# Moving the gating and normalisation of the DeltaNet heads from GpSimd to VectorE

## The chip, the cores and the metric

One core of a Trainium2 chip runs the whole program. The time is the device time of one execution in microseconds; the kernel before takes 1177.71 us, the median of three runs (1175.47 to 1178.70). The engines are TensorE (PE), VectorE (DVE), ScalarE (ACT), GpSimd (POOL) and the DMA queue of SyncE (SP). Each runs its own list of instructions in order and waits for others on semaphores.

## The reference, cut to what matters

Two mixer blocks follow each other. The change lies in the second, a gated DeltaNet over 512 tokens with 16 value heads of width 128. For each head it computes, token by token,

```python
o = ...                                       # chunked delta rule, (tokens, heads, 128)
o = rms_norm_2(o, norm_w) * jax.nn.silu(z)    # per token and head: o * rsqrt(mean(o*o) + 1e-6) * norm_w * silu(z)
y = o.reshape(bsz, t, nh * dh) @ w_out        # (512, 2048) @ (2048, 1024)
x = x + gate * y                              # gate: one row of 1024, from the condition
out = rms_norm_2(x, final_g)
```

All is float32. A float32 product on TensorE is made of three products of rounded high and low parts (`hi` and `lo`); so every weight block is rounded by ScalarE (`hi`) and the rest is subtracted by VectorE or GpSimd (`lo`) before use.

## The kernel before, in words

The second mixer works on two groups (`i` = 0, 1) of four head pairs (`j` = 0 to 3). A pair is walked in four chunks of 128 tokens (`c` = 0 to 3). The order is written out by hand for each engine; nothing plans it.

**A chunk.** PE multiplies with the running state `S`; DVE makes `R` from that (L2597), PE makes `w` (L1904), DVE scales it into `we` and `w_sb` (L2605, L2609), PE makes the state update (L1909) and the output (L1918), and DVE writes the chunk's output into `O[j % 2]` (L2632 or L2634, semaphore `o_ok`). `O` lies in the tile `es`. ACT takes the sum of squares of each output chunk (L2182, `osq_ok`).

**Fills.** Between these steps PE, ACT and DVE do the triangular inverse of the next pair (`doubled` on DVE, L2584 and L2589). The last pair of a group has no next one: there `fill` turns the finished heads, makes their `hi` and `lo` parts (`high`, `low`), and in group 1 begins the output product.

**A finished pair.** GpSimd gates it (`gate_heads`, L2366: z = z * O, 128x1024), makes the factor `rs` from the sums of squares (`norm_factor`, L2351 and L2354), and multiplies (`finish`, L2372: z = z * rs, 128x1024, `z_ok` + 8). `z` lies in the tile `tok`. PE turns heads e = 2j, 2j + 1 only when `z_ok` has their 8 (`turn_m`, L1925).

**GpSimd's other work.** It spreads the inverse's factors (`expand`, L1609), makes the decay steps (L2340, into `es`) and the masked products (L2407), and subtracts weight rests (`out_rest`, L1587, 128x2048).

**The end.** `partial` holds the output product of group 0's heads. GpSimd adds it, times the gate row, to the residual: `add_partial(t)`, two 128x1024 operations for each of four token blocks (L2379, L2381), three of them ahead of the last pair's gating. PE turns e = 14, 15, then needs weight rest 6 (`wo_lo[0]` = 4) for the second half of the output columns and rest 7 (`wo_lo[2]`) for its last quarter. DVE makes rest 6, GpSimd rest 7. DVE adds each finished output block (L2705, L2707).

Of the kernel before, what the change touches and what calls it, by code (L numbers as in the profile page):

```python
# [9 lines left out]
ALU = mybir.AluOpType  # L10
ACT = mybir.ActivationFunctionType

P = 128
# [62 lines left out]
class Phase(ExitStack):  # L76
# [14 lines left out]
    def sem(self, name):  # L91
        s = self.enter_context(self.nc.semaphore(f"{self.name}_{name}"))
        Phase.used.append(s.num)
        return s
# [1299 lines left out]
def second_mixer(nc, a, ahead, wba, wba_in, split, raw, masks, resid, row_f, modc, gain, small, z):  # L1394
# [7 lines left out]
    with ctx:  # L1402
# [150 lines left out]
        osq_ok = sem("osq_ok")  # L1553
        rs_ok = sem("rs_ok")
        heads_out = sem("heads_out")
        z_gated, z_ok = sem("z_gated"), sem("z_ok")
        m_g_in, row_g_in, x_in = sem("m_g_in"), sem("row_g_in"), sem("x_in")
        m_turned, m_hi_ok, m_lo_ok = sem("m_turned"), sem("m_hi_ok"), sem("m_lo_ok")
        wo_in = [sem(f"wo_in{r}") for r in range(2)]
# [522 lines left out]
        def _(act):  # L2082
# [231 lines left out]
            for e in (12, 13):  # L2314
                high(e, 13 - e)
            round_out(6, b_used, 1)
            round_out(7, o_made, NB * HB * TT)
            for e in (14, 15):
                high(e, 15 - e)
            for half_n in range(2):  # L2320
                cols = slice(half_n * COLS, (half_n + 1) * COLS)
                for t in range(TT):
                    n = TT * half_n + t
                    act.wait_ge(added, n + 1)
                    if n:
                        act.wait_ge(sum_ok, n)
                    nc.scalar.activation(scratch[0][:, cols], resid[:, t, cols], ACT.Square, scale=D_MODEL ** -0.5,  # L2327
                                         accum_out=halves[:, half_n, t:t + 1]).then_inc(sum_ok, 1)

        @block.gpsimd  # L2330
        def _(pool):
# [17 lines left out]
            def norm_factor(i, j):  # L2349
# [3 lines left out]
                pool.wait_ge(pool_s, at(i, 1, j, 3))  # L2353
                nc.gpsimd.tensor_tensor(rs[:, j % 2], ms[:],  # L2354
                                        half[:, 1, 0:2 * TT].rearrange("p (h c) -> p h c", c=TT), ALU.pow).then_inc(rs_ok, 1)

            def heads_z(i, j):

                return z[:, :, (i * HB + j) * 2 * P:(i * HB + j + 1) * 2 * P].rearrange("p c (h e) -> p h c e", h=2)

            def gate_heads(i, j):

                pool.wait_ge(o_ok, at(i, 4, j, 4))
                if i == 0 and j == 0:
                    pool.wait_ge(zp_out, TT * B_Z)
                nc.gpsimd.tensor_tensor(heads_z(i, j), heads_z(i, j), O[j % 2], ALU.mult).then_inc(z_gated, 1)  # L2366

            def finish(i, j):

                pool.wait_ge(rs_ok, at(i, 1, j, 1))  # L2370
                pool.wait_ge(z_gated, at(i, 1, j, 1))
                nc.gpsimd.tensor_tensor(heads_z(i, j), heads_z(i, j),  # L2372
                                        rs[:, j % 2].unsqueeze(3).broadcast_to([P, 2, TT, P]), ALU.mult).then_inc(z_ok, 8)

            def add_partial(t):

                if t:
                    pool.wait_ge(part_ok, 2 * t)
                nc.gpsimd.tensor_tensor(gated, partial[:, t, :], row_b, ALU.mult).then_inc(part_ok, 1)  # L2379
                pool.wait_ge(part_ok, 2 * t + 1)  # L2380
                nc.gpsimd.tensor_tensor(resid[:, t, :], resid[:, t, :], gated, ALU.add).then_inc(part_ok, 1)  # L2381

            def begin(i):
                if i:
# [10 lines left out]
            for i in range(NB):  # L2395
                for j in range(HB):
                    if j + 1 < HB:
                        log_decay_steps(i, j + 1)
                    if i and j == HB - 1:
                        out_rest(nc.gpsimd, pool, 3)  # L2400
                    pool.wait_ge(e_ok, at(i, 1, j, 1))
                    pool.wait_ge(kk_out, at(i, 2, j, 2))
                    if i == 0 and j == 0:

                        for b in range(2):
                            pool.wait_ge(spilled[b], 16 * (B_CONV // 2))
                    nc.gpsimd.tensor_tensor(PT[:, 8 * j:8 * j + 8, :].rearrange("p (h c) e -> p h c e", h=2),  # L2407
                                            E.rearrange("p (h c) e -> p h c e", h=2),
                                            KQm.unsqueeze(1).broadcast_to([P, 2, TT, P]), ALU.mult).then_inc(pt_ok, 1)
                pool.wait_ge(kss_ok, at(i, 1, HB - 1, 1))  # L2410
                nc.gpsimd.tensor_tensor(flat(rinv[:]), flat(kss[:]), half[:, 0, :], ALU.pow).then_inc(rinv_ok, 1)
                if i == 0:
                    for s in range(2):
                        w.rest(nc.gpsimd, pool, s, B_CONV + 3)
                pool.wait_ge(uc_ok, i * 2 + 1)
                pool.wait_ge(pt_ok, at(i, 1, HB - 1, 1))
                expand(i, 0, Uc, U[0], ux_ok)
                pool.wait_ge(uc_ok, i * 2 + 2)
                expand(i, 1, Tc, T, tx_ok)
                expand(i, 1, Uc, U[1], ux_ok)  # L2420
                out_rest(nc.gpsimd, pool, 4 * i)
                for j in range(HB):
                    if j:
                        gate_heads(i, j - 1)
                        norm_factor(i, j - 1)
                        finish(i, j - 1)
                    if j + 2 < HB:
                        expand(i, j + 2, Tc, T, tx_ok)
                        pool.wait_ge(w_made, at(i, 4, j, 4))
                        expand(i, j + 2, Uc, U[j % 2], ux_ok)  # L2430
                    if j == 1:
                        out_rest(nc.gpsimd, pool, 4 * i + 1)
                if i == 0:
                    begin(1)
                else:
                    pool.wait_ge(gate_out, 2)
                    pool.wait_ge(x_in, 16)
                    pool.wait_ge(yp_out, 2 * TT)
                    pool.wait_ge(z_ok, 8 * (NB * HB - 1))
                    for t in range(3):  # L2440
                        add_partial(t)
                gate_heads(i, HB - 1)
                norm_factor(i, HB - 1)
                finish(i, HB - 1)

            add_partial(3)
            out_rest(nc.gpsimd, pool, 7)
            for t in range(TT):
                pool.wait_ge(sum_ok, t + 1)
                nc.gpsimd.tensor_scalar(halves[:, 0, t:t + 1], halves[:, 0, t:t + 1], 1.0, EPS2, ALU.mult, ALU.add)\  # L2450
# [10 lines left out]
        def _(dve):  # L2461
# [130 lines left out]
            def chunk_part(i, j, c, fill):  # L2592
# [31 lines left out]
                fill(4 * c + 2)  # L2624
                dve.wait_ge(o_made, at(i, 4, j, c + 1))
                out = O[slot][:, :, c, :]
                if c == 0 and j >= 2:

                    dve.wait_ge(z_gated, at(i, 1, j - 2, 1))
                if c:  # L2630
                    dve.wait_ge(qt_ok, at(i, 6, j, 2 * c))
                    nc.vector.tensor_tensor(out, psO[:, 2:4, :], qt[:], ALU.add).then_inc(o_ok, 1)  # L2632
                else:
                    nc.vector.tensor_copy(out, psO[:, 2:4, :]).then_inc(o_ok, 1)  # L2634
                fill(4 * c + 3)

            def low(e, bank):
                dve.wait_ge(m_hi_ok, e + 1)
# [3 lines left out]
            def heads_of(i):  # L2642
# [21 lines left out]
                for j in range(HB):  # L2664
                    parts = doubling_parts(j + 1) if j + 1 < HB else None

                    def fill(n):
                        if parts:
                            if n < len(parts):
                                doubled(i, j + 1, *parts[n])  # L2670
                        elif n == 2:
                            for e in range(8 * i, 8 * i + 4):
                                low(e, 2 + e % 8)
                        elif i == 0 and n == 5:
                            select(1)
                        elif i and n == 0:
                            nc.vector.tensor_tensor(diag.rearrange("p (k c) -> p k c", c=P),
                                                    ident.unsqueeze(1).broadcast_to([P, KT, P]),
                                                    modc[:, 2 * KT:].unsqueeze(2).broadcast_to([P, KT, P]), ALU.mult)\
                                .then_inc(gate_in, 1)  # L2680

                    for c in range(TT):
                        chunk_part(i, j, c, fill)
                dve.wait_ge(o_ok, at(i, 4, HB - 1, 4))
                dve.sem_inc(heads_out, 1)
                for e in (12, 13) if i else (4, 5):
                    low(e, 13 - e if i else e - 2)

            for i in range(NB):
                heads_of(i)  # L2690
            out_rest(nc.vector, dve, 6)
            for e in (14, 15):
                low(e, 15 - e)

            def finish_row(t, halves=1):
                if t == 0:
# [7 lines left out]
            def add_gated(x, y, gate, n):  # L2704
                own.did(nc.vector.tensor_tensor(scratch[1][:, 0:n], y, gate, ALU.mult))  # L2705
                own.wait()
                return nc.vector.tensor_tensor(x, x, scratch[1][:, 0:n], ALU.add)  # L2707

            for half_n in range(2):
                cols = slice(half_n * COLS, (half_n + 1) * COLS)  # L2710
                for t in range(TT):
                    dve.wait_ge(acc_made, TT * half_n + t + 1)
                    if half_n or t:
                        dve.wait_ge(added, TT * half_n + t)
                    if half_n == 0:
                        dve.wait_ge(part_ok, 2 * (t + 1))
                    add_gated(resid[:, t, cols], ps[:, (2, 3, 4, 5, 6, 7, 0, 1)[TT * half_n + t], :], row_b[:, cols], COLS)\
                        .then_inc(added, 1)
                    if half_n and t in (1, 2):
# [54 lines left out]
```

## Time and profile before

| | |
|---|---|
| median of three runs | 1177.71 us (1175.47 to 1178.70) |
| the profiled execution | 1178.70 us, its span 1176.9 us |
| PE busy | 1117.6 us, 95% |
| DVE busy | 670.5 us, 57% |
| ACT busy | 465.5 us, 40% |
| POOL busy | 244.3 us, 21% |
| TensorE clock granted, mean | 0.982 |

The second mixer's head loops run from about 868 us to 956 us (group 0) and from about 1040 us to 1130 us (group 1); the end follows. A row of the timeline gives start, duration, engine, line, operation, output and inputs, and in brackets how long the engine sat idle before it and what released it. The `x2` or `x8` at a row's end are equal instructions merged into one row, from the first's start to the last's end.

### The profile page before, as it was taken

To read this page: it belongs to the slowest core of one execution; us is meant where nothing else is said; L and a number is where in the kernel's file an instruction comes from. 1 tells how busy PE (TensorE), PEld (TensorE's weight loads), DVE (VectorE), ACT (ScalarE), POOL (GpSimd) and SP (SyncE) were. 2 spreads that over 40 slices of the span, in tenths; PEclk is the share of its full clock that TensorE was granted. 3 is DMA by queue.
4 is the path that set the end of the run, shared out by engine and by line. 5 is a ranking of instruction groups with operands and counts; after the bars stand their busy time and mean duration, and the time that the engine had idled before them with its cause. 6 is when DMAs were issued, how large, how long until landed. Compare 5 with 4: busy or idle time off the path is not lost. (4 is left out here: it accounts for less than half of the span.)

```text
span 1176.9 us, 15099 instructions
## 1 busy us (share of the span) xinstructions
PE 1117.6 (95%) x5878; PEld 926.3 (79%) x5878; DVE 670.5 (57%) x1081; ACT 465.5 (40%) x853; POOL 244.3 (21%) x170
## 2 busy tenths in 40 slices
PE   6999999999899899897999999999999889999897
PEld 4888888888689777786787888777799877788785
DVE  3245437621366877458377576576635667845635
ACT  3222233331466532224233333476245446244531
POOL 0001000000000422012000000133434553436592
PEclk9999999999999899899999999999999989999999
DMA  8276524231310502233243453432211212111401
GB/s 281 74 266 240 172 89 161 72 107 53 126 55 19 184 1 72 91 106 109 84 143 115 165 186 108 142 126 90 72 55 55 90 37 90 36 57 53 161 2 71
DMA packets 58308, 124.06 MB, mean 105 GB/s; under 512 B 5760, under 2 KB 5888, under 8 KB 58112
## 3 DMA queue, kind: packets, MB, share of 16 engines
q1 hardware_dynamic: 55792, 110.22, 27.7%
q0 software_dynamic: 2304, 12.58, 2.9%
q8 instruction: 45, 0.74, 0.3%
q10 hardware_dynamic: 144, 0.33, 0.1%
q14 instruction: 23, 0.19, 0.1%
HBM read 108.96 MB, written 14.16 MB: 105 GB/s over the span
## 5 line engine op out<-in xcount | busy, mean ns | idle before, releaser
L285 DVE TENSOR_TENSOR w_lo<-raw,w_hi 128x2048 fp32r<-128x2048 f32 x56 | 130.3, 2328 | 222.3 <-ACT w_hi L281 211.2
L281 ACT ACTIVATE w_hi<-raw 128x2048 fp32r<-128x2048 f32 x51 | 97.6, 1913 | 228.4 <-PE projections_ps L131 148.3
L129 PE MATMUL projections_ps<-projections_x_hi,w_hi 128*128 128x512 f32 x224 | 88.1, 393 | 3.0 <-DVE w_lo L285 2.6
L131 PE MATMUL projections_ps<-projections_x_hi,w_lo 128*128 128x512 f32 x224 | 87.6, 391 | 0.0
L130 PE MATMUL projections_ps<-projections_x_lo,w_hi 128*128 128x512 f32 x224 | 87.6, 391 | 0.0
L129 PE MATMUL projections_ps<-w_hi,projections_x_hi 128*128 128x512 f32 x192 | 74.7, 389 | 0.0
L130 PE MATMUL projections_ps<-w_lo,projections_x_hi 128*128 128x512 f32 x192 | 74.7, 389 | 0.0
L131 PE MATMUL projections_ps<-w_hi,projections_x_lo 128*128 128x512 f32 x192 | 74.7, 389 | 0.0
L242 DVE SCALAR_TENSOR_TENSOR resid<-resid,mixer_cw 128x512 f32<-128x512 f32 x96 | 65.0, 745 | 0.0
L2340 POOL TENSOR_TENSOR mixer_es<-masks,mixer_gsel 128x1024 f32<-128x1024 f32 x8 | 15.4, 1927 | 235.4 <-DVE mixer_bsel L2511 210.7
L2589 DVE COPY_PREDICATED mixer_space<-mixer_masks,mixer_ps 128x512 f32<-128x512 int32 x48 | 35.6, 742 | 45.7 <-PE mixer_ps L1878 45.7
L129 PE MATMUL mixer_ps<-w_hi,mixer_ha_hi 128*128 128x512 f32 x128 | 55.7, 435 | 5.3 <-ACT tok L2112 2.3
L129 PE MATMUL output_ps<-w_hi,output_m_hi 128*128 128x512 f32 x128 | 54.1, 423 | 0.7 <-DVE output_m_lo L1233 0.6
L1171 POOL MEMSET output_half_neg<- 128x4 f32 x1 | 0.1, 101 | 260.1 <-POOLq L649 260.1
L129 PEld LDWEIGHTS projections_ps<-projections_x_hi,w_hi 128*128 128x128 f32 x224 | 42.4, 189 | 12.5 <-issue 3.1
L129 PE MATMUL mixer_ps<-mixer_ha_hi,w_hi 128*128 128x512 f32 x128 | 50.6, 395 | 0.9 <-DVE w_lo L285 0.5
L131 PE MATMUL mixer_ps<-w_hi,mixer_ha_lo 128*128 128x512 f32 x128 | 51.2, 400 | 0.0
L130 PE MATMUL mixer_ps<-w_lo,mixer_ha_hi 128*128 128x512 f32 x128 | 51.1, 399 | 0.0
L130 PE MATMUL output_ps<-w_lo,output_m_hi 128*128 128x512 f32 x128 | 50.9, 398 | 0.0
L131 PE MATMUL output_ps<-w_hi,output_m_lo 128*128 128x512 f32 x128 | 50.7, 396 | 0.0
L129 PE MATMUL mixer_ps<-mixer_hb_hi,w_hi 128*128 128x512 f32 x128 | 50.4, 394 | 0.0
L1878 PE MATMUL mixer_ps<-mixer_space 128*128 128x128 f32 x384 | 50.4, 275 | 0.0
(314 smaller groups left out, 2765.8 us busy)
## 6 DMA issues: line engine op xcount, KB each, us to landing
raw<-in_w_in SPq DMA_DIRECT2D x26, 1024.0 KB, 5.0
raw<-in_gdn_w_in SPq DMA_DIRECT2D x24, 1024.0 KB, 5.0
tok<-in_ada_w POOLq DMA_DIRECT2D x16, 768.0 KB, 6.3
raw<-in_w_out SPq DMA_DIRECT2D x8, 1024.0 KB, 5.0
qkv_kept<-mixer_ring SPq DMA_DIRECT2D x8, 1024.0 KB, 4.2
mixer_st<-qkv_kept SPq DMA_DIRECT2D x32, 256.0 KB, 3.0
raw<-in_gdn_w_out SPq DMA_DIRECT2D x8, 1024.0 KB, 5.2
resid<-in_att_bias SPq DMA_DIRECT2D x16, 256.0 KB, 2.7
```

The lines of the kernel that those rows point to most:

```text
L129: nc.tensor.matmul(out, w_hi, x_hi, start=first, stop=False, skip_group_check=True)
L130: nc.tensor.matmul(out, w_hi, x_lo, start=False, stop=False, skip_group_check=True)
L131: return nc.tensor.matmul(out, w_lo, x_hi, start=False, stop=last, skip_group_check=True)
L242: ins = nc.vector.scalar_tensor_tensor(out=acc, in0=src, scalar=tap, in1=acc, op0=ALU.mult, op1=ALU.add)
L281: self.nc.scalar.activation(self.hi[s][:], self.raw[s][:], ACT.Copy).then_inc(self.hi_ready, 1)
L285: engine.tensor_tensor(self.lo[s][:], self.raw[s][:], self.hi[s][:], ALU.subtract)\
L1171: nc.gpsimd.memset(half_neg[:], -0.5).then_inc(pool_step, 1)
L1878: mm = nc.tensor.matmul(out, V[:, m, :], U[j % 2][:, m, :], start=True, stop=True)
L2340: nc.gpsimd.tensor_tensor(steps, upper.unsqueeze(1).broadcast_to([P, 8, P]), gs.unsqueeze(2).broadcast_to([P, 8, P]), ALU.mult).then_inc(s ...
L2589: nc.vector.copy_predicated(U[j % 2][:, 4 * grp:4 * grp + 4, :], level.unsqueeze(1).broadcast_to([P, 4, P]), psZ[:, grp, :].rearrange("p ( ...
```

## The change

The two GpSimd passes over z are gone. In their place DVE does eight SCALAR_TENSOR_TENSOR operations of 128x128 for each pair, z = (O * rs) * z, one for each head and chunk; each adds 1 to `z_ok`. DVE does them for pair j - 1 after chunk 1 of pair j (j = 1 to 3), and for the last pair of a group after the two `low` that follow it. GpSimd keeps `norm_factor`. The semaphore `z_gated` goes, and DVE no longer waits for it before it reuses `O`. At the end GpSimd adds `partial` for t = 2 and 3 only, t = 2 after the last pair's `norm_factor`; DVE adds t = 0 and 1 after its last two `low`. Rest 6 goes from DVE to GpSimd, and ACT rounds unit 7 after `high` of 14 and 15.

```diff
@@ ACT, the end
             round_out(6, b_used, 1)
-            round_out(7, o_made, NB * HB * TT)
             for e in (14, 15):
                 high(e, 15 - e)
+            round_out(7, o_made, NB * HB * TT)
@@ GpSimd
                     if j:
-                        gate_heads(i, j - 1)
                         norm_factor(i, j - 1)
-                        finish(i, j - 1)
...
-                    for t in range(3):
-                        add_partial(t)
-                gate_heads(i, HB - 1)
                 norm_factor(i, HB - 1)
-                finish(i, HB - 1)
...
+            pool.wait_ge(z_ok, 8 * (NB * HB - 1))
+            add_partial(2)
+            for v in (6, 7):
+                out_rest(nc.gpsimd, pool, v)
+            pool.wait_ge(part_ok, 2)
             add_partial(3)
-            out_rest(nc.gpsimd, pool, 7)
@@ DVE
-                    dve.wait_ge(z_gated, at(i, 1, j - 2, 1))
...
+            def finish(i, j):
+
+                dve.wait_ge(rs_ok, at(i, 1, j, 1))
+                if i == 0 and j == 0:
+                    dve.wait_ge(zp_out, TT * B_Z)
+                for h in range(2):
+                    for c in range(TT):
+                        at_z = i * (2 * HB * P) + (2 * j + h) * P
+                        zz = z[:, c, at_z:at_z + P]
+                        nc.vector.scalar_tensor_tensor(out=zz, in0=O[j % 2][:, h, c, :], scalar=rs[:, j % 2, h, c:c + 1],
+                                                       in1=zz, op0=ALU.mult, op1=ALU.mult).then_inc(z_ok, 1)
...
                         chunk_part(i, j, c, fill)
+                        if c == 1 and j:
+                            finish(i, j - 1)
...
                     low(e, 13 - e if i else e - 2)
+                finish(i, HB - 1)
...
-            out_rest(nc.vector, dve, 6)
             for e in (14, 15):
                 low(e, 15 - e)
...
+            for t in range(2):
+                own.wait()
+                own.did(add_gated(resid[:, t, :], partial[:, t, :], row_b, D_MODEL))
```

DVE before, around the end of chunk 1 of a pair with j = 1 to 3 (L2619 is the state, L2632 the output of the chunk into `es`, L2597 is `R` of the next chunk):

```order
L2619 SCALAR_TENSOR_TENSOR mixer_S<-mixer_S,mixer_dsel,mixer_ps 128x128 x2
L2632 TENSOR_TENSOR mixer_es<-mixer_ps,mixer_qt 128x2x128
L2597 SCALAR_TENSOR_TENSOR mixer_R<-mixer_ps,mixer_dsel,mixer_vr 128x128 x2
```

The same place after; the lines are numbered anew, L2595, L2605 and L2573 are the three from above:

```order
L2595 SCALAR_TENSOR_TENSOR mixer_S<-mixer_S,mixer_dsel,mixer_ps 128x128 x2
L2605 TENSOR_TENSOR mixer_es<-mixer_ps,mixer_qt 128x2x128
L2619 SCALAR_TENSOR_TENSOR tok<-mixer_es,mixer_rs,tok 128x128 x8
L2573 SCALAR_TENSOR_TENSOR mixer_R<-mixer_ps,mixer_dsel,mixer_vr 128x128 x2
```

The eight new operations stand between a chunk's output and the next chunk's `R`.

GpSimd before, from the gating of pair 2 of group 1 to the last weight rest:

```order
L2366 TENSOR_TENSOR tok<-tok,mixer_es 128x2x4x128
L2351 TENSOR_TENSOR mixer_ms<-mixer_sums,mixer_qe 128x8
L2354 TENSOR_TENSOR mixer_rs<-mixer_ms,mixer_half 128x8
L2372 TENSOR_TENSOR tok<-tok,mixer_rs 128x2x4x128
L2379 TENSOR_TENSOR mixer_es<-tok,mixer_Tc 128x1024
L2381 TENSOR_TENSOR resid<-resid,mixer_es 128x1024
```

(twice more L2379 and L2381, then L2366, L2351, L2354, L2372, L2379, L2381 and rest 7.) After, from the factor of the last pair on:

```order
L2351 TENSOR_TENSOR mixer_ms<-mixer_sums,mixer_qe 128x8
L2354 TENSOR_TENSOR mixer_rs<-mixer_ms,mixer_half 128x8
L2411 TENSOR_TENSOR mixer_es<-tok,mixer_Tc 128x1024
L2413 TENSOR_TENSOR resid<-resid,mixer_es 128x1024
L1587 TENSOR_TENSOR w_lo<-raw,w_hi 128x2048
L1587 TENSOR_TENSOR mixer_w_lo<-raw,mixer_w_hi 128x2048
L2411 TENSOR_TENSOR mixer_es<-tok,mixer_Tc 128x1024
L2413 TENSOR_TENSOR resid<-resid,mixer_es 128x1024
```

The first addition of `partial` now follows the last pair's factor, and rest 6 follows that.

DVE after, from the `low` of 12 and 13 to the first output block; the kernel before has rest 6 where L2619 stands, and neither of the four 128x1024 rows:

```order
L2624 SCALAR_TENSOR_TENSOR mixer_hb_lo<-mixer_ps,mixer_m_g,mixer_hb_hi 128x512 x2
L2619 SCALAR_TENSOR_TENSOR tok<-mixer_es,mixer_rs,tok 128x128 x8
L2624 SCALAR_TENSOR_TENSOR mixer_hb_lo<-mixer_ps,mixer_m_g,mixer_hb_hi 128x512 x2
L2695 TENSOR_TENSOR mixer_ktok<-tok,mixer_Tc 128x1024
L2697 TENSOR_TENSOR resid<-resid,mixer_ktok 128x1024
L2695 TENSOR_TENSOR mixer_ktok<-tok,mixer_Tc 128x1024
L2697 TENSOR_TENSOR resid<-resid,mixer_ktok 128x1024
L2695 TENSOR_TENSOR mixer_ktok<-mixer_ps,mixer_Tc 128x512
```

## Rows read from the trace of the kernel before

**Rows 1.** The page, busy time of the engines.
```profile
PE 1117.6 (95%) x5878; PEld 926.3 (79%) x5878; DVE 670.5 (57%) x1081; ACT 465.5 (40%) x853; POOL 244.3 (21%) x170
```

**Rows 2.** The waits of PE, 860 to 1177 us: total, times, longest.
```profile
PE mixer_ps L1850 <- DVE mixer_space L2589: 4.8, 6, 0.9
```

**Rows 3.** Timeline of DVE, group 0, pair 2, chunks 1 and 2.
```profile
923.61 0.42 DVE L2632 TENSOR_TENSOR mixer_es<-mixer_ps,mixer_qt 128x256 f32<-128x256 f32 x1 [0.73 <-PE mixer_ps L1918]
924.94 0.61 DVE L2597 SCALAR_TENSOR_TENSOR mixer_R<-mixer_ps,mixer_dsel,mixer_vr 128x128 f32<-128x128 f32 x2 [0.90 <-PE mixer_ps L1887]
...
926.89 0.41 DVE L2605 TENSOR_TENSOR mixer_we<-mixer_ps,mixer_wsce 128x256 f32<-128x256 f32 x1
927.22 0.42 DVE L2609 TENSOR_TENSOR mixer_w_sb<-mixer_ps,mixer_wsc 128x256 f32<-128x256 f32 x1
```

**Rows 4.** Timeline of PE, the same chunk.
```profile
926.06 0.61 PE L1904 MATMUL mixer_ps<-mixer_R,mixer_space 128*128 128x128 f32 x4
```

**Rows 5.** Timeline of DVE, two operations with both inputs in SBUF.
```profile
1172.99 1.42 DVE L2701 SCALAR_TENSOR_TENSOR resid<-resid,row_f,mixer_Uc 128x512 f32<-128x512 f32 x2 [0.71 <-POOL row_f L2458]
```

**Rows 6.** Timeline of DVE, group 0, pair 3, chunks 1 and 2.
```profile
944.93 0.42 DVE L2632 TENSOR_TENSOR mixer_es<-mixer_ps,mixer_qt 128x256 f32<-128x256 f32 x1 [0.25 <-PE mixer_ps L1918]
946.00 0.61 DVE L2597 SCALAR_TENSOR_TENSOR mixer_R<-mixer_ps,mixer_dsel,mixer_vr 128x128 f32<-128x128 f32 x2 [0.64 <-PE mixer_ps L1887]
```

**Rows 7.** Timelines of DVE and PE, group 1, pair 3, chunks 1 and 2.
```profile
1119.74 0.42 DVE L2632 TENSOR_TENSOR mixer_es<-mixer_ps,mixer_qt 128x256 f32<-128x256 f32 x1 [0.53 <-PE mixer_ps L1918]
1120.87 0.61 DVE L2597 SCALAR_TENSOR_TENSOR mixer_R<-mixer_ps,mixer_dsel,mixer_vr 128x128 f32<-128x128 f32 x2 [0.70 <-PE mixer_ps L1887]
...
1121.80 0.61 PE L1904 MATMUL mixer_ps<-mixer_R,mixer_space 128*128 128x128 f32 x4
```

**Rows 8.** Timelines of POOL, DVE and PE: group 1, pair 3, start; last, an undisturbed DVE row.
```profile
1107.33 2.37 POOL L2366 TENSOR_TENSOR tok<-tok,mixer_es 128x1024 f32<-128x1024 f32 x1 [10.15 <-DVE mixer_es L2632]
...
1108.19 2.58 DVE L2677 TENSOR_TENSOR mixer_space<-masks,modc 128x1024 f32<-128x1024 f32 x1
...
1111.17 0.70 PE L1909 MATMUL mixer_ps<-mixer_we,mixer_ktok 128*128 128x256 f32 x2 [1.21 <-DVE mixer_we L2605]
...
995.68 1.22 DVE L2540 TENSOR_TENSOR resid<-mixer_space,mixer_nbp 128x1024 f32<-128x1024 f32 x1
```

**Rows 9.** Timelines of POOL, DVE and PE between the two groups.
```profile
960.42 1.90 POOL L2372 TENSOR_TENSOR tok<-tok,mixer_rs 128x1024 f32<-128x1024 f32 x1
...
962.59 1.60 DVE L2526 SCALAR_TENSOR_TENSOR mixer_nbp<-mixer_bsel,mixer_r 128x8 f32<-128x8 f32 x1
...
971.43 1.96 PE L1839 MATMUL mixer_ps<-mixer_es,masks 128*128 128x512 f32 x4 [0.94 <-DVE mixer_hb_lo L2639]
```

**Rows 10.** Timelines of ACT, POOL, DVE and PE at the end.
```profile
1130.31 0.19 ACT L2182 ACTIVATION_READ_ACCUMULATOR mixer_junk<-mixer_es 128x1 f32 x1
...
1134.47 1.92 ACT L2194 ACTIVATE w_hi<-raw 128x2048 fp32r<-128x2048 f32 x1 [2.66 <-PE mixer_ps L131]
...
1134.87 1.64 POOL L2354 TENSOR_TENSOR mixer_rs<-mixer_ms,mixer_half 128x8 f32<-128x8 f32 x1
1136.65 3.82 POOL L2372 TENSOR_TENSOR tok<-tok,mixer_rs 128x1024 f32<-128x1024 f32 x1
...
1136.42 2.29 DVE L1587 TENSOR_TENSOR w_lo<-raw,w_hi 128x2048 fp32r<-128x2048 f32 x1 [3.75 <-ACT w_hi L2194]
...
1140.53 1.09 PE L1925 MATMUL mixer_ps<-masks,tok 128*128 128x128 f32 x8 [0.55 <-POOL tok L2372]
1141.38 0.48 PE L129 MATMUL mixer_ps<-w_hi,mixer_ha_hi 128*128 128x512 f32 x1
```

**Rows 11.** Line L1587 on POOL: duration ns min/median/max, first and last start.
```profile
L1587 POOL TENSOR_TENSOR w_lo<-raw,w_hi x5: 4527/4534/4566, 870.1 to 1086.4; 128x2048 fp32r<-128x2048 f32 x5
```

**Rows 12.** Timeline of PE at its earlier wait for ACT.
```profile
757.52 0.50 PE L129 MATMUL mixer_ps<-w_hi,mixer_ha_hi 128*128 128x512 f32 x1 [2.27 <-ACT tok L2112]
```

**Rows 13.** Windows of PE: stretch, length, busy (count), PEclk, DMA share, GB/s.
```profile
757.00:767.00 10.00, 9.48 (x43) 0.83 0.37 135
```

More of the change, by code:

```diff
@@ L1555, in second_mixer @@
         heads_out = sem("heads_out")
-        z_gated, z_ok = sem("z_gated"), sem("z_ok")
+        z_ok = sem("z_ok")
         m_g_in, row_g_in, x_in = sem("m_g_in"), sem("row_g_in"), sem("x_in")
@@ L2355, in norm_factor @@
                                         half[:, 1, 0:2 * TT].rearrange("p (h c) -> p h c", c=TT), ALU.pow).then_inc(rs_ok, 1)
[L2357 to L2381, printed above, removed]
             def begin(i):
@@ L2434, in _, with add_partial @@
                     begin(1)
[L2435 to L2439, printed above, removed]
-                    for t in range(3):
-                        add_partial(t)
-                gate_heads(i, HB - 1)
-                norm_factor(i, HB - 1)
-                finish(i, HB - 1)
+                norm_factor(i, HB - 1)
+            def add_partial(t):
+                nc.gpsimd.tensor_tensor(gated, partial[:, t, :], row_b, ALU.mult).then_inc(part_ok, 1)
+                pool.wait_ge(part_ok, 2 * (t - 2) + 1)
+                nc.gpsimd.tensor_tensor(resid[:, t, :], resid[:, t, :], gated, ALU.add).then_inc(part_ok, 1)
+            pool.wait_ge(gate_out, 2)
+            pool.wait_ge(x_in, 16)
+            pool.wait_ge(yp_out, 2 * TT)
+            pool.wait_ge(z_ok, 8 * (NB * HB - 1))
[3 more added lines that the diff above has]
+            pool.wait_ge(part_ok, 2)
             add_partial(3)
-            out_rest(nc.gpsimd, pool, 7)
             for t in range(TT):
@@ L2626, in chunk_part @@
                 out = O[slot][:, :, c, :]
-                if c == 0 and j >= 2:
-                    dve.wait_ge(z_gated, at(i, 1, j - 2, 1))
                 if c:
@@ L2687, in heads_of @@
                     low(e, 13 - e if i else e - 2)
+                finish(i, HB - 1)
             for i in range(NB):
                 heads_of(i)
-            out_rest(nc.vector, dve, 6)
             for e in (14, 15):
                 low(e, 15 - e)
+            dve.wait_ge(gate_out, 2)
+            dve.wait_ge(x_in, 16)
+            dve.wait_ge(yp_out, 2 * TT)
             def finish_row(t, halves=1):
@@ L2707, in add_gated @@
                 return nc.vector.tensor_tensor(x, x, scratch[1][:, 0:n], ALU.add)
+            for t in range(2):
+                own.wait()
+                own.did(add_gated(resid[:, t, :], partial[:, t, :], row_b, D_MODEL))
+            own.wait()
             for half_n in range(2):
@@ L2714, in _ @@
                         dve.wait_ge(added, TT * half_n + t)
-                    if half_n == 0:
-                        dve.wait_ge(part_ok, 2 * (t + 1))
+                    if half_n == 0 and t >= 2:
+                        dve.wait_ge(part_ok, 2 * (t - 1))
                     add_gated(resid[:, t, cols], ps[:, (2, 3, 4, 5, 6, 7, 0, 1)[TT * half_n + t], :], row_b[:, cols], COLS)\
```

## The prediction

> **What bounds the kernel now.** I read the page first: PE is busy for 1117.6 of 1176.9 us, DVE for 670.5, POOL for 244.3 [rows 1]. So the end is set by PE's own work and by the few places where PE stands still; taking work off POOL or putting it on DVE matters only where PE then waits less or more. The waits of PE from 860 us on are therefore the second view: the largest group is the turn of the next pair's values behind DVE's predicated copy, 4.8 us in six waits [rows 2], and the change touches neither side of it. Third, the timelines at the places where the new order differs. They show a head loop in which PE runs nearly without a gap, and DVE answers each PE step in a gap of its own of 0.5 to 1 us. Last comes the end of the program, where PE waits 0.55 us for POOL's last pass over z [rows 10].
>
> **Head loops: what is added.** DVE gets eight 128x128 operations with both inputs in SBUF for each of eight pairs. [...] The pairs of 128x128 in the loop, fed from PSUM, take 0.61 us together [rows 3]; with about 0.34 for one that is a step of 0.26 to 0.27. I take 0.257, eight make 2.06 us. [...]
>
> Pairs 1 and 2 of each group: the chunk's output starts at 923.61; the next instruction can start 0.34 later, as L2609 does behind L2605 (926.89 to 927.22) [rows 3], at 923.95. The eight end their issue at 926.01, `R` then takes 0.61 to 926.62, and PE's product can start at 926.67. It started at 926.06 [rows 4], since `R` had a gap of 0.90 us ahead of it. PE loses 0.61 us, and it has no later gap of its own that could give this back: its 0.9 us wait at the pair's end [rows 2] follows from its own product and DVE's copy. Four such pairs: 4 x 0.61 = 2.44.
>
> Pair 3 has no fill work, so the chain of PE and DVE alone sets it. Group 0: output at 944.93, eight done at 944.93 + 0.34 + 2.06 = 947.33, `R` had started at 946.00 [rows 6]: +1.33. Group 1: 1119.74 + 2.40 = 1122.14, `R` ends at 1122.75, PE at 1122.81 and not 1121.80 [rows 7]: +1.01.
>
> The factor `rs` is there in time: POOL, without its passes over z, has it several us before the end of chunk 1. The last pair of a group is finished while PE does other work.
>
> **Head loops: what is removed.** One DVE operation is stretched by a pass that goes. L2677, 128x1024, starts at 1108.19, while POOL's gating runs from 1107.33 to 1109.70; it takes 2.58 us against 1.22 for the same size undisturbed, and PE then waits 1.21 us for the operation behind it [rows 8]. Without the pass PE can go on when its transposes end, at 1109.80 and not 1111.17: -1.37. What follows in that chunk hangs on DVE and moves with it. Between the groups POOL's second pass ends at 962.32 and its decay steps follow at once, so a tiny DVE operation of 128x8 takes 1.60 us [rows 9]. DVE now waits for the factor (about 958.7), does its eight until 960.8, and the steps on POOL come some 0.9 us sooner. DVE's chain ends about 0.8 us earlier, where PE waited 0.94 us [rows 9]: -0.8, between 0 and -0.94. Sum of the loops: 2.44 + 1.33 + 1.01 - 1.37 - 0.8 = +2.6.
>
> **The end.** POOL's 7.1 us of additions ahead of the last gating go, but it now stands idle until the last sums of squares, which end at 1130.50 [rows 10]. From there: the factor, 1.64 and a short sum ahead of it [rows 10], to 1132.5; `add_partial(2)`, two operations of 128x1024 at 2.37 and a gap [rows 8], to 1137.4; rest 6, 4.53 on POOL [rows 11], to 1142.0. ACT has rounded it by 1136.4 [rows 10], so POOL's own queue is what is late. DVE's eight start at the same moment as `add_partial(2)`. That the two engines hold each other off is shown by the last pass over z: 3.82 us instead of 1.90, since DVE's L1587 had started 0.23 us before it and ran until 1138.71 [rows 9, 10]. So the 2.06 us of DVE are added wherever they fall: rest 6 is there at 1144.1.
> PE ends its products at 1139.98, turns heads 14 and 15 in 0.85 us, and went on at 1141.38 [rows 10]. It now goes on at 1144.1: +2.7. Lower bound: no clash on the port, 1142.1, +0.7; upper: POOL gets in between the eight and the last `z_ok` comes at 1143.6, with the transposes still to do, +3.1.
> [...]
> Rest 7 on POOL and DVE's four additions (4 x 1.22, rows 8) also share the port, from 1143 to about 1157, but rest 7 is needed only at 1158 and later, and DVE's first output block can be late by nearly 2 us before PE's pace of 2.8 us for each later block is missed: 0, at most +1.
>
> **The clock.** [...] The new wait at the end is about 3.2 us, behind which PE has only products: +1.7, at least 0, at most twice that.
>
> **Sum.** +2.6 + 2.7 + 1.7 = +7.0 on the profiled execution's 1178.7: 1185.7. That execution is 1.0 above the median, so 1184.7 for a median.
>
> **Rivals.**
> A, forecast: all of this, 1184.7; own range 1182 to 1188. For it: the gaps in rows 3 and 4 are smaller than the eight.
> B, no fall of the clock at the end: 1177.7 + 5.3 = 1183.0. For it: the transposes split the wait into parts.
> C, the port isn't held, or DVE's eight come in POOL's gaps: end +0.7, no fall: 1177.7 + 3.3 = 1181.0. Against it the 3.82 us.
> D, not slower: the step of the eight is at most 0.19 us. Then they take 1.55 us, `R` ends 0.5 us earlier than reckoned, pairs 1 and 2 cost 0.1 each, the two pairs 3 cost 0.8 and 0.5, in all 1.7 against 2.2 won; with the end as in C, 1178. The point from which it decides: a step under 0.2 us. [...]
> [...]
> E, faster: D, and the two reliefs (2.2 us) and the lost POOL wait (0.55) count in full, and DVE's eight hide in pair 3 too: about 1175, or less where a slow stretch of the clock goes with a wait. It needs rest 6 in time, against the sum of POOL's own queue.
> F, the change doesn't do what it says, for instance the eight do not sit on PE's path because the chunk's product is late for another reason: 1178 to 1179.
>
> **How the numbers follow.** A 0.44, B 0.12, C 0.13, D 0.15, E 0.10, F 0.06. About 0.3% (3.5 us) is what a measurement of this kernel can tell from no change. Slower by more: A, B and two thirds of C, 0.65. Within: the rest of C, D, F, and a little of E, 0.26. Faster by more: 0.09. Range: from 1177, which leaves out E, to 1188, A with its upper bounds.
>
> **What would show it.** Right: DVE's row of eight takes about 2.1 us, PE's L1904 of chunk 2 is released by `R` with a wait of 0.6 us in pairs 1 and 2 and over 1 us in pair 3; L2677 is back near 1.2 us; PE waits about 3 us around its turn of heads 14 and 15 for POOL's or DVE's work, and the clock falls behind it. Wrong: a row of eight under 1.6 us, no new waits before L1904, or rest 6 done on POOL before PE asks.

## The result, and the profile after

The kernel after takes 1185.39 us (median of four runs, 1183.45 to 1187.27), the kernel before in the same comparison 1178.01 us (1175.47 to 1178.70). The ratio is 1.0064, with a 95% interval of 1.0047 to 1.0083: slower, by more than this measurement can mistake. The forecast was +7.0 us, the medians say +7.4. The profiled execution took 1185.66 us, its span is 1183.9.

The page of after, answering [rows 1]:

```profile
PE 1120.3 (95%) x5878; PEld 927.8 (78%) x5878; DVE 702.8 (59%) x1148; ACT 465.7 (39%) x853; POOL 205.6 (17%) x151
```

POOL lost 38.7 us of work and DVE took 32.3. PE's own work grew by 2.7 us though it does the same products: some of them ran at a granted clock of 0.50, shown below. The rest of the loss is standing still. The waits of PE from 860 us on (total, times, longest), to be laid beside [rows 2]:

```profile
PE mixer_ps L1850 <- DVE mixer_space L2565: 4.8, 6, 0.9
PE mixer_ps L1904 <- DVE mixer_R L2573: 4.0, 6, 1.2
PE mixer_ps L1890 <- DVE mixer_es L2607: 4.0, 2, 2.3
PE mixer_ps L1925 <- DVE tok L2619: 3.4, 1, 3.4
...
PE mixer_ps L1909 <- DVE mixer_we L2581: 1.0, 2, 0.5
```

The same view of before, its rows that differ:

```profile
PE mixer_ps L1909 <- DVE mixer_we L2605: 2.2, 3, 1.2
...
PE mixer_ps L1839 <- DVE mixer_hb_lo L2639: 0.9, 1, 0.9
...
PE mixer_ps L1904 <- DVE mixer_R L2597: 0.2, 1, 0.2
```

The first and third row of after are as before. New are six waits for `R` (4.0 us; before it was one of 0.2) and one for the last pair's finished heads (3.4, where before waited 0.55 for POOL [rows 10]). The 1.2 us behind L2677 and the 0.9 between the groups are gone.

**The loops.** DVE and PE of after, group 0, pair 1, chunks 1 and 2 (start, duration, engine, line); it answers to [rows 3, 4]:

```profile
901.07 0.42 DVE L2605 TENSOR_TENSOR mixer_es<-mixer_ps,mixer_qt 128x256 f32<-128x256 f32 x1 [0.73 <-PE mixer_ps L1918]
901.41 2.18 DVE L2619 SCALAR_TENSOR_TENSOR tok<-mixer_es,mixer_rs,tok 128x128 f32<-128x128 f32 x8
903.51 0.60 DVE L2573 SCALAR_TENSOR_TENSOR mixer_R<-mixer_ps,mixer_dsel,mixer_vr 128x128 f32<-128x128 f32 x2
...
904.16 0.71 PE L1904 MATMUL mixer_ps<-mixer_R,mixer_space 128*128 128x128 f32 x4 [0.48 <-DVE mixer_R L2573]
```

The row of eight starts 0.34 us after the chunk's output and takes 2.18 us; one alone takes 0.346 (the line's median), so the step is (2.18 - 0.346) / 7 = 0.262 us. `R` follows 2.10 us after the row's start. PE then waits 0.48 us. In the pairs 3, which have no inverse of a next pair to fill the gaps, the same wait is longer. Group 0's and group 1's, against [rows 6, 7] of before:

```profile
950.29 0.71 PE L1904 MATMUL mixer_ps<-mixer_R,mixer_space 128*128 128x128 f32 x4 [1.21 <-DVE mixer_R L2573]
...
1123.09 0.71 PE L1904 MATMUL mixer_ps<-mixer_R,mixer_space 128*128 128x128 f32 x4 [0.87 <-DVE mixer_R L2573]
```

The relief is there too: L2677 of [rows 8], now L2662, runs undisturbed, and PE no longer waits behind it.

```profile
1109.82 1.21 DVE L2662 TENSOR_TENSOR mixer_space<-masks,modc 128x1024 f32<-128x1024 f32 x1
```

**The end.** POOL, DVE and PE of after, to be read against [rows 10]:

```profile
1132.25 1.64 POOL L2354 TENSOR_TENSOR mixer_rs<-mixer_ms,mixer_half 128x8 f32<-128x8 f32 x1
1133.85 2.40 POOL L2411 TENSOR_TENSOR mixer_es<-tok,mixer_Tc 128x1024 f32<-128x1024 f32 x1
1136.33 2.41 POOL L2413 TENSOR_TENSOR resid<-resid,mixer_es 128x1024 f32<-128x1024 f32 x1
1138.69 4.60 POOL L1587 TENSOR_TENSOR w_lo<-raw,w_hi 128x2048 fp32r<-128x2048 f32 x1
...
1133.99 10.77 DVE L2619 SCALAR_TENSOR_TENSOR tok<-mixer_es,mixer_rs,tok 128x128 f32<-128x128 f32 x8
1149.46 5.59 DVE L2697 TENSOR_TENSOR resid<-resid,mixer_ktok 128x1024 f32<-128x1024 f32 x1
...
1144.82 1.97 PE L1925 MATMUL mixer_ps<-masks,tok 128*128 128x128 f32 x8 [3.44 <-DVE tok L2619]
```

The same eight operations take 2.18 us in the loop and 10.77 us here. POOL's three operations beside them have their undisturbed durations (2.40, 2.41, 4.60), while the first three of DVE's eight took 2.40, 2.56 and 4.64 us, one beside each of POOL's three, and the other five 0.34 us each. So in this row each of those three ended 0.1 to 0.15 us behind one of POOL's, POOL's next one went ahead of DVE's next, and DVE's row ended only when POOL's three were through. PE waits 3.44 us for it. The prediction and the expectations call what the engines hold from each other the port, as does a heading below; the traces show the holding, by these durations, and not what lies behind it.

The clock at the end of that wait and behind it, in windows of PE (stretch, length, busy, granted clock); it answers to [rows 13]:

```profile
1144.00:1154.00 10.00, 9.18 (x32) 0.66 0.01 2
1150.00:1160.00 10.00, 10.00 (x43) 0.96 0.00 0
```

Windows of 1 us have a granted clock of 0.50 from 1144 to 1150 and of 1.00 from 1151, so a mean of 0.66 over 10 us is 6.8 us at 0.50 and 3.2 at 1.00. The stretch began inside the wait, at about 1143.9 (from 1143 to 1145 the mean is 0.73), some 2.5 us after PE's last product had ended, so about 0.9 of its 6.8 us were spent waiting. In the other 5.9 us PE lost 2.7 against before.

### The profile page after: what moved, and what is told of

The parts are those of the page before. It is cut to its first block, busy times and chain, and to the rows that moved or that the text cites. A ratio compares the mean times of both kernels' runs of the same rounds, so it can differ in the third digit from the quotient of the medians.

```text
span 1183.9 us, 15137 instructions
## 1 busy us (share of the span) xinstructions
PE 1120.3 (95%) x5878; PEld 927.8 (78%) x5878; DVE 702.8 (59%) x1148; ACT 465.7 (39%) x853; POOL 205.6 (17%) x151
## 4 chain that ended last, share of the span: by engine, by line
PE 41%; DVE 7%; issue 2%; ACT 2%; POOL 1%; DVEq 0%; POOLq 0%; ACTq 0%
PE mixer_ps L129 8%; PE mixer_ps L131 8%; PE mixer_ps L130 8%; PE mixer_ps L1878 3%; PE mixer_ps L1876 3%; DVE tok L2619 2%; PE mixer_ps L1904 2%; DVE resid L242 1%; PE mixer_ps L1918 1%; PE mixer_ps L1909 1%; PE mixer_ps L1830 1%; PE mixer_ps L1880 1%; PE mixer_ps L1839 1%; POOL w_lo L285 1%; PE mixer_ps L1890 1%
## 5 line engine op out<-in xcount | busy, mean ns | idle before, releaser
L1876 PE MATMUL mixer_ps<-mixer_space,resid 128*128 128x128 f32 x384 | 50.3, 275 | 0.0
```

What stands on the lines that cost most here:

```text
L1876: mm = nc.tensor.matmul(out, C[:, 8 * j + m, :], T[:, m, :], start=True, stop=True)
```

## The experiments

Each was timed beside the kernel before on the same chip; the ratio is always to before (1177.69 us for the first four, 1177.46 for the last four). First come the parts of the end, then those of the loops, then a version with both parts mended.

### Rest 6 ahead of the additions

```diff
-            pool.wait_ge(z_ok, 8 * (NB * HB - 1))
+            out_rest(nc.gpsimd, pool, 6)
+            pool.wait_ge(z_ok, 8 * (NB * HB))
             add_partial(2)
-            for v in (6, 7):
-                out_rest(nc.gpsimd, pool, v)
+            out_rest(nc.gpsimd, pool, 7)
```

> The changed kernel with GpSimd's end in another order: rest 6 first, then the additions for t = 2, held until the last pair's eight operations on VectorE are done (z_ok = 64). Theory (GpSimd's queue and the shared port make the end late): rest 6 is done about 4.6 us after ScalarE has rounded it, VectorE's eight take 2.2 us instead of 10.8, PE waits under 0.6 us around the turn of heads 14 and 15 instead of 3.4, the clock stays at full rate there, and the time falls by 5 to 6 us against the changed kernel, to a ratio of about 1.001 to 1.002 to the kernel before. Rival (the loss of the end comes from VectorE's own four additions or from ScalarE's later rounding of unit 7): less than 1 us is won, ratio near 1.006.

1181.21 us, ratio 1.0039 (1.0024 to 1.0054). The waits at the end shrink to 0.44 us, and the clock stays up. DVE and PE, then a window of PE:

```profile
1131.14 2.19 DVE L2619 SCALAR_TENSOR_TENSOR tok<-mixer_es,mixer_rs,tok 128x128 f32<-128x128 f32 x8
1146.53 5.52 DVE L2695 TENSOR_TENSOR mixer_ktok<-tok,mixer_Tc 128x1024 f32<-128x1024 f32 x1
1155.43 0.69 DVE L2695 TENSOR_TENSOR mixer_ktok<-mixer_ps,mixer_Tc 128x512 f32<-128x512 f32 x1
...
1139.84 0.47 PE L129 MATMUL mixer_ps<-w_hi,mixer_ha_hi 128*128 128x512 f32 x1 [0.44 <-POOL w_lo L1587]
```

```profile
1136.00:1146.00 10.00, 9.56 (x46) 1.00 0.01 2
```

So a good part of the end's loss, about 3 us by the two ratios, was the order of POOL's queue and what it did to DVE. It gave back less than the end had cost, and missed its expected ratio of 1.001 to 1.002, since the next thing was already late: DVE's own four additions, in clashes with POOL's rest 7 and `add_partial` 2.10, 3.31, 5.52 and 3.31 us long, push the first output block to 1155.43. From there it has no gap for 10 us: PE's last product starts 1.55 us earlier than in before (1167.68 against 1169.23), and DVE's last operation ends 0.6 us later. Beside these long operations POOL is held too: its rest 7 takes 5.59 us where it took 4.58 before. In after the same additions cost nothing, since PE was later still.

### The port free, the queue as it is

```diff
-            pool.wait_ge(z_ok, 8 * (NB * HB - 1))
+            pool.wait_ge(z_ok, 8 * (NB * HB))
             add_partial(2)
```

> The changed kernel, only that GpSimd's additions for t = 2 wait until the last pair's eight are done (z_ok = 64); its order stays: additions, then rest 6. Theory (the sum of GpSimd's queue counts, not who gets the port first): VectorE's eight take 2.2 us, but rest 6 is now done 4.6 + 4.9 us behind them, at about 1145.6 us on the trace's clock, so PE waits 3.4 us for rest 6 instead of for z_ok; the time is within 1 us of the changed kernel, ratio 1.005 to 1.006. Rival (only the starving of VectorE's row at the port counts): the wait is gone and 5 us are won, ratio near 1.002.

1185.87 us, ratio 1.0073 (1.0053 to 1.0093): no gain. DVE, POOL and PE:

```profile
1133.99 2.18 DVE L2619 SCALAR_TENSOR_TENSOR tok<-mixer_es,mixer_rs,tok 128x128 f32<-128x128 f32 x8
...
1141.18 4.51 POOL L1587 TENSOR_TENSOR w_lo<-raw,w_hi 128x2048 fp32r<-128x2048 f32 x1
...
1145.84 0.47 PE L129 MATMUL mixer_ps<-w_hi,mixer_ha_hi 128*128 128x512 f32 x1 [3.60 <-POOL w_lo L1587]
```

The eight are back at 2.18 us, heads 14 and 15 turn at once, and PE waits 3.60 us for rest 6 instead. In both kernels PE can go on only when eight operations on DVE and three on POOL, which hold each other off, are through; which of them goes first changed the name of the wait and hardly its length (3.44 and 3.60 us). The stretched row of 10.77 us is thus a symptom, and the long queue of POOL the cause.

### The eight left out of the loops

```diff
-                            finish(i, j - 1)
+                            dve.wait_ge(rs_ok, at(i, 1, j - 1, 1))
+                            dve.sem_inc(z_ok, 8)
```

> The changed kernel with the eight operations left out for all pairs but the last of each group (VectorE only waits for the factor and signals z_ok), so those heads of z are not gated nor normalised. Theory (the eight stand on PE's path): PE's six waits for R, 4.0 us, go, and the time falls by 3.0 to 4.6 us against the changed kernel, ratio 1.003 to 1.004; group 0's slow stretch of the clock may be longer again and take back 1.7 us of it. Rival (PE gives the delay back at its next wait for VectorE anyway): under 1 us is won, ratio near 1.006.

The edit leaves those heads of z neither gated nor normalised, so it only shows a cost. 1177.63 us, ratio 1.0013 (0.9996 to 1.0029): the loop's eight are worth about 0.5%, 6 us, by intervals that don't exclude the 4.0 us of their waits. For `R` the list of waits has one of 0.2 us left, as before; the wait at the end is unchanged. Below it stand the windows of PE around that wait and behind it:

```profile
PE mixer_ps L1925 <- DVE tok L2619: 3.4, 1, 3.4
```

```profile
1132.00:1142.00 10.00, 6.56 (x33) 1.00 0.01 2
1138.00:1148.00 10.00, 10.00 (x44) 1.00 0.01 2
```

But in this execution the clock did not fall behind the 3.44 us. The twelve runs lie in two clusters: seven from 1175.17 to 1177.76 us with a mean granted clock of 0.984 or more, five from 1180.22 to 1183.51 us with 0.979 or less. The profiled execution is one of the first; a fall in the others would explain the second cluster, but none of them has a trace.

### The eight of pairs 1 and 2 behind chunk 3

```diff
-                        if c == 1 and j:
+                        if c == (1 if j == HB - 1 else TT - 1) and j:
                             finish(i, j - 1)
```

> The changed kernel with the eight of pairs 1 and 2 moved from behind chunk 1 to behind chunk 3, where VectorE sat idle 1.25 us for PE's turn of the next values; pair 3 stays. Theory (the cost is the eight minus the gap in which they stand, minus PE's slack): the four waits of PE for R of 0.5 us go and none comes in their place, since the next values are needed by PE only 2 us later: 2.0 to 2.4 us are won against the changed kernel, ratio 1.004 to 1.005. Rival (the cost is the same 2.2 us wherever the row stands): no change, with new waits at the start of pairs 2 and 3.

1197.89 us, ratio 1.0176 (1.0156 to 1.0196): 13 us slower than after. The expectation looked at the gap in DVE and not at what POOL does at that moment. POOL and DVE, group 0, pair 1, and PE behind them:

```profile
908.80 2.49 POOL L1609 TENSOR_TENSOR mixer_space<-mixer_Uc,mixer_masks 128x512 f32<-128x512 f32 x2
911.25 4.56 POOL L1587 TENSOR_TENSOR w_lo<-raw,w_hi 128x2048 fp32r<-128x2048 f32 x1
...
910.39 7.15 DVE L2619 SCALAR_TENSOR_TENSOR tok<-mixer_es,mixer_rs,tok 128x128 f32<-128x128 f32 x8
...
918.52 1.22 PE L1909 MATMUL mixer_ps<-mixer_we,mixer_ktok 128*128 128x256 f32 x2 [4.58 <-DVE mixer_we L2581]
```

POOL's operations again have their own durations. Of DVE's eight the first two took 1.05 and 4.60 us, the others 0.34 each, and the row ends 1.7 us after the weight rest, at 917.54. PE's waits for `we` over both groups, of which after has 1.0 us:

```profile
PE mixer_ps L1909 <- DVE mixer_we L2581: 10.6, 5, 4.6
```

In pair 2, where POOL is idle, the row takes 2.18 us, and PE waits 1.34 us for the heads it is to turn next. Chunk 1 was not a bad place: it is one at which POOL is silent.

### The change's loops with the old kind of end

```diff
@@ POOL, the end
+            add_partial(0)
+            add_partial(1)
+            norm_factor(NB - 1, HB - 1)
+            pool.wait_ge(z_ok, 8 * (NB * HB))
             add_partial(2)
-            for v in (6, 7):
-                out_rest(nc.gpsimd, pool, v)
-            pool.wait_ge(part_ok, 2)
+            out_rest(nc.gpsimd, pool, 7)
             add_partial(3)
...
@@ DVE, the end
+            out_rest(nc.vector, dve, 6)
             for e in (14, 15):
                 low(e, 15 - e)
...
-            for t in range(2):
-                own.wait()
-                own.did(add_gated(resid[:, t, :], partial[:, t, :], row_b, D_MODEL))
```

ACT has its old order back too. The semaphore waits that go with all this are not shown.

> The changed kernel with the head loops left as changed and the end put back near the kernel before: VectorE makes rest 6 and adds no partial, GpSimd adds t = 0 and 1 ahead of the last pair's factor, waits for the last pair's eight, then adds t = 2, rest 7, t = 3; ScalarE's order is the old one. Theory (loops and end are two separate losses, +2.6 and about +4.4 with the clock): no wait of PE over 0.5 us around heads 14 and 15, VectorE's eight take 2.2 us, the six waits for R (4.0 us) stay; the time is 5 to 7 us under the changed kernel, ratio 0.999 to 1.002. Rival (the port clash only moves, and GpSimd's additions or VectorE's rest 6 now bind the end): a new wait over 2 us there and a ratio over 1.004.

1178.59 us, ratio 1.0009 (0.9994 to 1.0023). Of after's 0.64% the end was 0.55%, 6.5 us. DVE:

```profile
1133.68 2.19 DVE L2624 SCALAR_TENSOR_TENSOR tok<-mixer_es,mixer_rs,tok 128x128 f32<-128x128 f32 x8 [0.30 <-POOL mixer_rs L2354]
1137.13 3.38 DVE L1587 TENSOR_TENSOR w_lo<-raw,w_hi 128x2048 fp32r<-128x2048 f32 x1 [1.26 <-ACT w_hi L2194]
```

POOL adds its first two blocks before the last factor, and waits out DVE's eight; PE stands still for nothing at heads 14 and 15. DVE's rest 6 is held for 1.1 us (3.38 against 2.29 in [rows 10]), which delays nobody. The six waits for `R` (4.0 us) are all still there, and the ratio is near 1 all the same: by the sum, the two reliefs pay for them.

### The eight spread over the gaps of chunk 1

```diff
+            SPREAD = ({4: (0, 2), 5: (2, 1), 6: (3, 2), 7: (5, 3)}, {4: (0, 4), 5: (4, 1), 6: (5, 1), 7: (6, 2)})
...
+                        filled(n)
+                        if j and n in SPREAD[j == HB - 1]:
+                            finish(i, j - 1, *SPREAD[j == HB - 1][n])
...
-                        if c == 1 and j:
-                            finish(i, j - 1)
```

The rest is the kernel just told of; `n` is the gap in DVE's order, four to a chunk, and the pair of numbers says which of the eight go into it.

> The kernel with the new end, and the eight operations of each pair handed out in pieces of 1 to 4 to the idle gaps of VectorE in chunk 1 of the next pair (2, 1, 2, 3 in pairs 1 and 2; 4, 1, 1, 2 in pair 3), where GpSimd is idle too. Theory (PE pays only for what exceeds a gap and its own slack): PE's four waits for R of 0.5 us go, those of pair 3 shrink under 0.5 us, 3 to 4 us are won against the new end alone, ratio 0.996 to 0.999, so at or under the kernel before. Rival (each piece delays the chain by its full length, as the gaps are part of the chain): the waits stay at 4 us in sum, spread over L1904, L1909 and L1918, and nothing is won.

1175.41 us, ratio 0.9973 (0.9960 to 0.9986). DVE in group 0, pair 1, chunk 1:

```profile
899.33 0.61 DVE L2627 SCALAR_TENSOR_TENSOR tok<-mixer_es,mixer_rs,tok 128x128 f32<-128x128 f32 x2
900.23 0.42 DVE L2586 TENSOR_TENSOR mixer_we<-mixer_ps,mixer_wsce 128x256 f32<-128x256 f32 x1 [0.28 <-PE mixer_ps L1904]
...
903.12 0.87 DVE L2627 SCALAR_TENSOR_TENSOR tok<-mixer_es,mixer_rs,tok 128x128 f32<-128x128 f32 x3
904.11 0.61 DVE L2578 SCALAR_TENSOR_TENSOR mixer_R<-mixer_ps,mixer_dsel,mixer_vr 128x128 f32<-128x128 f32 x2
```

Two operations fit into a gap and DVE still stands idle for 0.28 us before its next step. No wait for `R` is left among PE's longer ones. The eight are the same operations in the same chunk: 0.36%, 4.2 us, is what their place costs, and the sum of the six waits is 4.0.

### The `low` of group 0 apart, in that kernel and in the kernel before

In both kernels PE's L1890 waits 4.0 us in two waits, the longer of them 2.3, behind four `low` in a row on DVE, in the pairs 3. This edit takes those of group 0 apart:

```diff
-                        elif n == 2:
+                        elif i == 0 and n in (3, 8, 9, 12):
+                            e = (3, 8, 9, 12).index(n)
+                            low(e, 2 + e)
+                        elif i and n == 2:
```

With the spread eight:

> The spread kernel, and in the last pair of group 0 the four operations low (2.7 us on VectorE ahead of the copy of chunk 0's output) handed out one by one behind chunk 0's output, R of chunk 2, w_sb of chunk 2 and R of chunk 3. Theory (PE's wait of 2.3 us there is VectorE's row of four, and the slow stretch of the clock follows that wait): the wait at L1890 falls under 0.3 us, the granted clock stays 1.0 from 938 to 956 us, and 3 to 5 us are won, ratio 0.992 to 0.996. Rival (the slow stretch comes from PE being thinly used in that pair, not from that one wait): the wait goes, but the clock still falls, and only 1 to 2 us are won.

1171.00 us, ratio 0.9937 (0.9921 to 0.9954): faster than both kernels of this case. In the kernel before:

> The kernel before with only the four low of group 0's last pair handed out in the same way. Theory: the same 3 to 5 us as for the kernel with spread operations, ratio 0.996 to 0.997, so this gain has nothing to do with where z is gated. Rival (it needs the free port): GpSimd's passes over z stretch nothing here, since low reads only one operand from SBUF, so no difference is expected; if one shows, ratio over 0.999.

1173.01 us, ratio 0.9961 (0.9948 to 0.9974). The waits of PE from 860 us on, with the spread eight first, then before:

```profile
PE mixer_ps L1909 <- DVE mixer_we L2586: 2.2, 2, 1.7
PE mixer_ps L1890 <- DVE mixer_es L2612: 1.7, 1, 1.7
```

```profile
PE mixer_ps L1890 <- DVE mixer_es L2634: 1.7, 1, 1.7
...
PE mixer_ps L1887 <- DVE mixer_S L2619: 1.2, 1, 1.2
```

The wait of 2.3 us is gone in each, and a shorter one stands elsewhere (1.71 us at L1909 and 1.2 us at L1887). The gain of 0.4% is more than that exchange. The granted clock fits the rest: over all executions its median is 0.980 with the spread eight alone (nine) and 0.984 with this edit (six), 0.981 in before (26) and 0.985 with the edit (twelve), and 0.004 of 1175 us is an estimate of 4.7 us. Windows of PE at this place, first before and after:

```profile
930.00:960.00 30.00, 24.91 (x142) 0.83 0.12 36
```

```profile
930.00:960.00 30.00, 23.80 (x145) 0.89 0.11 36
```

Then the change's loops with the old kind of end, and the spread eight, both without this edit:

```profile
930.00:960.00 30.00, 23.89 (x137) 0.83 0.11 36
930.00:960.00 30.00, 24.87 (x142) 0.83 0.12 36
```

Last the two kernels with the edit, the spread eight first:

```profile
925.00:945.00 20.00, 17.46 (x113) 0.91 0.08 27
```

```profile
930.00:950.00 20.00, 15.66 (x102) 1.00 0.12 41
```

The slow stretch is 10.2 us long in before (0.17 x 2 x 30, at a granted clock of 0.50), 6.6 in after, 10.2 in the two kernels without the edit, 3.6 with the spread eight and the edit, and none in before with the edit. So the clock did not stay up throughout, as was expected for the spread eight: it still fell at a wait, the one of 1.71 us. And the loops of after, with the same waits for `R` and for the `low`, have 6.6 us in one execution and 10.2 in another. Against before with the same edit, the change with its eight spread and its end mended is another 0.2% faster; the two intervals overlap a little. GpSimd's passes did not stretch `low` in the kernel before: its 16 took 0.735 to 0.751 us each, two of them (from 956.12) beside L2366 (956.06 to 958.42).

## Why the prediction was right

The sum, 7.0 us, is the measured shift of PE's last product in the two traces, 1169.23 to 1176.23. The parts, by the starts of the same PE operations in the two:

- **The eight in the pairs 1 and 2**, forecast 0.61 us each: the shift was 0.07 us ahead of group 0's first row of eight, 0.76 behind it, and stood at 1.42 at the start of pair 3, so 0.68 each. Right, and with it the step (0.257 taken as an estimate, where the pairs of [rows 3] gave 0.26 to 0.27; 0.262 measured). Rival D falls by its own point of decision, 0.2 us: no run shows its step of 0.19. How much of the step is length, a line of the same kind says: L2701 of before took 1.28 us at 128x1024 and 0.746 at 128x512, so 0.53 for 512 elements and, as an estimate from that, 0.13 for 128. About half of the 0.262 us is thus fixed, as are 0.14 of the 0.67 us (1.42 less 0.746) by which the two of [rows 5] follow each other.
- **The pairs 3**, +1.33 and +1.01: the second grew the shift from 0.25 to 1.29, so +1.04. In group 0 the wait for `R` was there (1.21 us), but the shift at the group's end was 1.10, less than the 1.42 at its pair's start. What it lost it got back from the clock: the slow stretch there was 6.6 us long and not 10.2, worth about 1.7. The forecast had no such term, and it was luck: the same loops with the old kind of end had 10.2 us again.
- **The reliefs**, -1.37 and -0.8: L2662 takes 1.21 us and the wait behind it is gone; in group 1 the shift went from 0.27 to 1.63 over the pairs 1 and 2, and behind L2662 it is 0.25: -1.38. Between the groups the shift fell from 1.10 to 0.28, -0.82. The tiny operation that was to be relieved there was still stretched (1.76 us, 128x8, L2502), so the path to that number was partly wrong. The relieved one was another, two ahead of it: of 128x4 elements, it took 1.89 us beside POOL's second pass (L2522 of before) and takes 0.17 now, so DVE's chain came forward.
- **The end**, +2.7, upper bound +3.1: PE's products before the turn end 1.40 us later than before (1141.38 against 1139.98), the turn starts 4.29 later. So the end's wait added 2.89 us, between the two. It came in the way of the upper bound: POOL got in between the eight, and PE waited for `z_ok`, not for rest 6, which was done at 1143.29. The forecast had the queue of POOL right and the engine that is held wrong. The rows of 10.77 us (here) and 7.15 us (behind chunk 3) show POOL's operations going ahead between single ones of DVE's eight, until POOL's large ones were done.
- **The clock**, +1.7, at most twice that: the 1.7 is (1 - 0.83) x 10 us, from the window of [rows 13] behind the wait of 2.27 us [rows 12], where windows of 1 us have 0.50 from 758 to 761 and 1.00 from 762. The shift grew from 4.29 to 7.0 behind the turn, +2.7. The size was off: the slow stretch was 6.8 us and not 3.4, 5.9 of them with PE at work. Rival B (no fall) did not happen in this execution, but it did in the one without the eight in the loops, behind the same 3.44 us. So one such wait was followed by a fall and the other was not.

Two errors cancel: the loops ended at +1.40 and not +2.6, and the clock cost +2.7 and not +1.7; the end added 0.2. The additions on DVE, costed at nothing, were indeed absorbed, but two of them took 3.30 us and one 5.59 where 1.22 were reckoned, DVE's first output block was 7.5 us later than before (1161.77 against 1154.27), and DVE had its first gap only at the fifth block (0.55 us). That was luck of a late PE: where PE was on time, as with rest 6 ahead, they held up the end.

Of the other rivals, C falls (the row of eight was held, 10.77 us instead of 2.18), E and F fall with the six new waits. What stays open is when a wait brings the clock down, and for how long: behind one of 3.44 us a trace shows 6.8 us of slow clock, another none. Nor is the clock the same far from any edit. A window of PE near the start of the program, where all kernels are alike, in before and in the kernel without the eight in the loops:

```profile
12.00:22.00 10.00, 7.73 (x28) 0.83 0.95 320
```

```profile
12.00:22.00 10.00, 8.96 (x40) 1.00 1.01 342
```

The first has 3.4 us at a granted clock of 0.50 there, 1.7 us of work lost, the second none. So the spans of two single profiles differ by a few us that belong to no edit; the ratios above are of medians.

## What to carry to other kernels

Work moved from an idle engine to a busier one cost here about what its row is longer than the gap it stands in, less the slack of the engine that waits (0.68 us for a row of 2.10 with some 1.0 of gap and 0.45 of slack), as long as GpSimd did not hold it up; so cut it into pieces of the gaps' size (4.2 us won with the same operations). Before a row of short VectorE operations like these, with both inputs in SBUF, is put anywhere, look what GpSimd runs at that time: twice here GpSimd got in between its operations, and the row lasted until GpSimd's large operations were through (7.15 and 10.77 us instead of 2.18). And at the end of a program, sum up each engine's queue from its last input on: the order within it only names the wait, unless something that nobody waits for is moved behind what PE needs.

## What was not expected of the hardware

- Eight operations of 128x128 took 2.18 us alone, 7.15 and 10.77 us beside back-to-back GpSimd operations, which themselves were not slowed (2.40, 2.41 and 4.60 us; 2.37 and 4.53 in the kernel before).
- A 128x1024 addition on VectorE took 1.22, 2.10, 3.30, 5.52 or 5.59 us, by what GpSimd did beside it.
- A stretch of TensorE's granted clock at 0.50 in the same pair of the same group lasted 10.2, 6.6 or 3.6 us or didn't come. Part of that goes with the waits, moved by one or two us: breaking up one of 2.3 us went with a median clock 0.004 higher. Part is chance, since the same loops had 6.6 us in one execution and 10.2 in another.
